# The second block's first modulation product, with 32 stationary columns in four partition groups for 64 in two

## What is computed

```python
def second_block(x, c, ada_w, ada_b, ...):
    cond = jax.nn.silu(c)                                  # 1 x 1024
    for layer in range(2):
        mod = (jnp.dot(cond, ada_w[layer]) + ada_b[layer])[:, None, :]   # 1024 x 6144
        sh1, sc1, g1, sh2, sc2, g2 = jnp.split(mod, 6, axis=-1)
        u = x * (1.0 + sc1) + sh1
        mix = _mixer(u, ...)
        x = _layernorm(ALPHA * x + (1.0 + g1) * mix, ...)
        u = x * (1.0 + sc2) + sh2
        ff = dense or mixture of experts, by layer
        x = _layernorm(ALPHA * x + (1.0 + g2) * ff, ...)
```

## Time and profile before

| | us |
|---|---|
| median of 3 runs | 2465.17 |
| lowest, highest | 2464.88, 2468.07 |
| the profiled execution | 2463.09 |
| its span, first to last instruction | 2461.4 |

### The profile page before, as it was taken

One profiled execution on the slowest core, in us unless ns is written; L12 is line 12 of the kernel. 1 busy time (PEld: TensorE's weight loads), 2 busy tenths in 40 slices (PEclk: granted clock), 3 DMA queues, 4 the chain that ended last, 5 costly groups with the idle time before them and its releaser, 6 DMA issues.

```text
span 2461.4 us, 68582 instructions
## 1 busy us (share of the span) xinstructions
PE 2197.1 (89%) x31915; PEld 1811.6 (74%) x31915; DVE 694.4 (28%) x1496; ACT 141.7 (6%) x270; POOL 160.5 (7%) x196
## 2 busy tenths in 40 slices
PE   6699989999999979779997977898898989899895
PEld 2478687777767768447764844798898979798895
DVE  7765242222222231343324224201011010101013
ACT  1101010000000000100000010000000000000000
POOL 8970000000000000000000000000000000000000
PEclk8899969999999969789998987899999999899998
DMA  9953569999999983237656322498988989898881
GB/s 345 301 180 120 189 208 353 394 395 394 394 395 394 394 297 128 95 133 257 247 205 222 120 103 81 160 335 308 336 301 301 327 305 343 299 347 302 313 313 67
DMA packets 304875, 658.36 MB, mean 267 GB/s; under 512 B 19844, under 2 KB 40852, under 8 KB 304660
## 3 DMA queue, kind: packets, MB, share of 16 engines
q1 hardware_dynamic: 295072, 646.99, 71.9%
q0 software_dynamic: 1456, 5.24, 0.7%
q10 hardware_dynamic: 8132, 2.72, 0.5%
HBM read 653.88 MB, written 1.05 MB: 266 GB/s over the span
## 4 chain that ended last, share of the span: by engine, by line
PE 78%; DMA 8%; DVE 6%; issue 5%; SPq 1%; ACT 1%; DVEq 0%; ACTq 0%
PE ps L1432 77%; DMA ring<-in_w_down_dram 8%; DVE arena L771 2%; PE ps L1440 2%; SPq L320 1%; DMA x<-in_x_dram 0%; DVE stat L870 0%; ACT hT L543 0%; DVE arena L1315 0%; ACTq L494 0%; DVE x L848 0%; DVE x L879 0%; DVE x L850 0%; DVEq L771 0%; DVE arena L1365 0%
## 5 line engine op out<-in xcount | busy, mean ns | idle before, releaser
L1432 PE MATMUL ps<-arena,ring 128*64 128x96 f32 (+2 forms) x25216 | 1010.5, 242 | 73.9 <-issue 70.4
L1432 PEld LDWEIGHTS ps<-arena,ring 128*64 128x64 f32 (+1 forms) x25216 | 991.1, 140 | 101.0 <-issue 95.3
L1432 PE MATMUL ps<-hT,ring 128*128 128x256 f32 x1616 | 353.5, 382 | 19.6 <-ACT hT L543 19.6
L1432 PEld LDWEIGHTS ps<-hT,ring 128*128 128x128 f32 x1616 | 308.6, 191 | 61.9 <-DVE stat L813 17.9
L1432 PE MATMUL ps<-ring,arena 128*64 128x512 f32 (+1 forms) x880 | 285.0, 616 | 17.4 <-DMA ring<-in_w_down_dram 14.9
L1432 PE MATMUL ps<-arena 128*128 128x128 f32 (+7 forms) x1296 | 242.2, 359 | 26.9 <-DVE arena L1143 11.4
L1168 DVE TENSOR_TENSOR arena<-arena,ps 128x384 f32<-128x384 f32 (+1 forms) x80 | 38.5, 481 | 741.3 <-PE ps L1432 741.3
L1432 PEld LDWEIGHTS ps<-ring,arena 128*64 128x64 f32 (+1 forms) x880 | 109.1, 164 | 175.2 <-issue 171.4
L1432 PEld LDWEIGHTS ps<-arena 128*128 128x128 f32 (+4 forms) x1296 | 166.7, 202 | 81.5 <-issue 50.4
L596 ACT ACTIVATE arena<-ps 128x384 f32<-128x384 f32 (+1 forms) x80 | 34.5, 432 | 1289.6 <-PE ps L1432 1289.6
L459 POOL TENSOR_SCALAR arena<-arena,starts,relD 128x256 f32<-128x256 f32 x64 | 92.1, 1446 | 9.2 <-DVE arena L737 5.9
(11 more groups left out here) (300 smaller groups left out, 892.0 us busy)
## 6 DMA issues: line engine op xcount, KB each, us to landing
ring<-in_moe_w_gate_dram SPq DMA_DIRECT2D x40, 2048.0 KB, 9.5
ring<-in_moe_w_up_dram SPq DMA_DIRECT2D x40, 2048.0 KB, 9.6
ring<-in_moe_w_down_dram SPq DMA_DIRECT2D x40, 2048.0 KB, 9.4
ring<-in_w_gate_dram SPq DMA_DIRECT2D x32, 2048.0 KB, 19.8
ring<-in_w_up_dram SPq DMA_DIRECT2D x32, 2048.0 KB, 19.7
ring<-in_w_down_dram SPq DMA_DIRECT2D x32, 2048.0 KB, 19.0
ring<-in_w_in_dram SPq DMA_DIRECT2D x18, 2048.0 KB, 10.5
ring<-in_w_ada_dram SPq DMA_DIRECT2D x12, 2048.0 KB, 20.4
```

The costliest lines, as they stand in the source:

```text
L1432: ins = pe.matmul(*args, **kw)
```

## The change

`ada_chunks` cuts each block of 128 features into four quarters of 32 columns, which go to partitions 0, 32, 64 and 96 of the same column of the same bank, where it cut it into two halves of 64. A chunk then has 128 matmuls in place of 64, or 256 recorded pairs in place of 128. Loops, slots, banks, semaphores, loads and what DVE reads stay as they are.

```diff
+QUARTER = 32
...
                     for f in range(4):
                         for k in range(KD):
-                            for c in range(2):
-                                at = f * P + c * HALF
-                                last = mm(ps[c * HALF:(c + 1) * HALF, bank, f:f + 1],
-                                          slot(s, KD, CH)[:, k, at:at + HALF], csT[:, 1, k:k + 1],
+                            for c in range(4):
+                                at = f * P + c * QUARTER
+                                last = mm(ps[c * QUARTER:(c + 1) * QUARTER, bank, f:f + 1],
+                                          slot(s, KD, CH)[:, k, at:at + QUARTER], csT[:, 1, k:k + 1],
                                           start=(k == 0), stop=(k == KD - 1))
```

## The result

| us | before | after |
|---|---|---|
| median (runs) | 2466.62 (4) | 2504.07 (4) |
| lowest, highest | 2464.88, 2474.83 | 2500.83, 2510.45 |
| profiled execution | 2463.09 | 2500.83 |
| its span | 2461.4 | 2499.1 |

A forecast was written before the change was run, and what follows sets the result against it. TensorE was taken to bound the kernel, with every chunk on the path. Pairs (+22.9 us) and code stalls (+19.3) made +42.2 on the profiled 2463.09, 2505.3; that run lying 2.1 below the median, 2507.4 was predicted, range 2484 to 2535.

The forecast's parts named there:

- A packet for 128 pairs: In all chunks, one instruction packet was to hold 128 pairs, so a chunk's code goes from one packet to two.
- the floor: In the chunks, issuing a weight load and a matmul was to take 29.9 ns a pair at either clock.
- the low bound: In the chunks, a pair's time goes with its columns: 15 ns at full clock, 26.7 at half, less if four loads overlap.
- rival 3: In the chunks, four loads overlap and code keeps ahead: 6.7 ns a pair at full clock, 13.3 at half; -31 us, 2434; 5%.
- The pairs' term: Over all twelve chunks, twice the pairs at 29.9 ns each were to add 22.9 us.
- The price of a stall: In chunks under weight loads, TensorE was to wait 1.9 us for each packet asked for; +19.3 us together.
- with the DMA mostly idle it costs nothing: In chunks without weight loads, such as chunk 2, fetching the added code was to bring no stall.
- If a chunk at half clock gets shorter: In chunks at 1.2 GHz, a shorter time was to show the forecast wrong in the main; about 9.5 us was expected under load.
- chunks at or under 3.8 us: In the changed profile, chunks this short were to be the sign of rival 3.
- 1 (code in time): In the chunks, code arrives in time and only the pairs count: +22.9 us, 2488; 15%.
- 2 (53.3 ns whatever the width): In chunks at half clock, a pair costs 53.3 ns at any width and nothing stalls: +81 us, 2546; 12%.
- 4: In the chunks, pairs go with their columns, two loads overlap, no stall: no difference, about 2466; 4%.

The follow-up runs named there:

- doubled halves: The kernel before with its halves of 64 columns, each sum made twice, so a chunk has 256 pairs; 2554.03 us.
- the best edit: Against the kernel before: condition column stationary, 128 weight columns moving, four partition groups, plus 110 small idle transposes ahead of the second expert loop; 2438.36 us, 0.9877.
- shifted: The kernel before with 18 extra small transposes (36 instructions) where TensorE waits, ahead of the second expert loop; 2480.9 us, 1.0056.
- the loop of two passes: The changed kernel with each chunk's quarters in a hardware loop run twice with the same results, one small matmul ahead and one behind; 2554.59 us.

## Why the prediction was right, and where it was wrong

- **The path.** Right: a chunk is on the path for all its length, nothing ahead absorbs the delay, behind chunk 12 next to nothing changes. +37.1 us at the transposes, +37.7 at the end of the span.
- **A packet for 128 pairs.** Right, to the packet: 12 more for 1536 more pairs. The Trainium skill, Runtime: NRT & Kernel Launch, Instruction fetch mechanics, gives blocks of 256 instructions fetched one after the other; this agrees (a packet for 128 recorded pairs of two instructions). Its "mostly hidden", which the prediction weighed, doesn't hold here: 63.7 us of stalls.
- **The price of a pair.** Wrong, and the step that failed is the floor: 29.9 ns for two forms was read as a floor on issuing. It was column time divided by the groups, and a rest of 2.4 to 4.7 ns at full clock that stays unexplained. Measured were 9.1 and 14.7 ns, below the low bound of 15 and 26.7 and near rival 3's 6.7 and 13.3. The pairs' term is -30.5 us for +22.9. The mechanism of rival 3 was true in this half. The prediction had read the half clock's 53.3 ns as column time; at full clock the same law gives 26.7, and the floor was built on the 3.2 ns that are missing, and on a second form that has 64 stationary columns as well.
- **The price of a stall.** Wrong in size by its use of the first: it took a packet's 5.7 us under load less 3.8 us of pairs. The distance was right (measured mostly 5.5 to 6.5 under load, up to 6.8), but the pairs fill 1.2 to 1.9 of it, so a stall is 4 to 5.4 us. And "with the DMA mostly idle it costs nothing" was wrong, as a packet then takes some 3.6 us, 1.5 to 2.5 of them idle. The row it was read from, the pairs of 29.8 ns from 363.06, could not show this: 128 of those last 3.8 us, just longer than the packet. Stalls come to 63.7 us together, for 19.3.
- **Why the sum held.** The terms are off by -53.4 and +44.4 us, and cancel to within 9. That is not luck alone: a cheaper pair only moves time from pairs to stalls, and the prediction had said so ("the packets then set the pace"; some 12 us less for a pair of 20 ns). It is luck in this: a later chunk was to take 5.7 us for a packet and 3.8 for pairs of 29.9 ns, and took 6.2 and 3.3 to 3.9, the second a packet as well. The wrong price of a pair came out near the time of a packet without load, which the prediction had not read anywhere. So chunks 9 to 12 came out at 38.1 for 38.2. Chunks 1 to 3, and 7 and 8, took 7.5 us less than forecast: in 1 and 3 the first 240 to 256 pairs had no gap in them, and 7 and 8 had a DMA share of 0.41. The lower clock behind the stalls adds about 3, within the 0 to 4 left for it.
- **The sign by which it would be wrong.** "If a chunk at half clock gets shorter" didn't occur. Yet "chunks at or under 3.8 us" for rival 3 couldn't show it, since the stalls hide it. The pair's time within a run of pairs was the sign to name.
- **The rivals.** 1 (code in time) falls with the gaps; 2 (53.3 ns whatever the width) with 14.7; 4 with both. 3 was right on the array and wrong on the code, and the forecast the other way round.

Still open: what makes a packet come at 3.6 and at 6 us (the DMA's own time or the queueing behind weights), the 6 us in the second expert loop with doubled halves, and the rest of a pair's time at full clock. A loop over the chunk's own blocks, so that its code stays at hand, was not tried as a version of its own.

## What to carry to other kernels

Of straight code made of very small matmuls count the packets: 128 pairs each, some 6 us under weight loads and some 3.6 without, and a stretch is the longer of its pairs and its packets, less the packets that are at hand when it starts (two here). To use the array's groups, give each instruction more to do (128 moving columns, four groups, a column of one as the stationary side) rather than cut the same work into more of them; here the granted clock stayed higher as well. And whoever adds or removes code ahead of a hot loop looks at how many instructions stand in its first packet before judging the edit: it was worth 10 to 13 us here, beside 29 us for the best edit.

## What the runs showed that was not expected

- Loads of the stationary side in four partition groups overlap nearly fourfold: 107 ns a pair of 64 columns in one group, 14.7 of 32 in four, at half clock. The Trainium skill, TensorEngine Tiling (Array Packing), Theoretical Speedup, gives up to 4x for a small side of at most 32. Per column it is 1.67 to 0.46 ns here, 3.6x, so the trace comes near it.
- At a DMA share of 0.02 packets of code still come only every 3.5 to 4.0 us, and under weight loads mostly every 5.5 to 6.5.
- A loop's place in its packets costs 2.3 to 2.4 us a pass in the mean of six, with the same instructions inside: 109.9 us before, 112.2 shifted.
- In the loop of two passes the second had no gap at all: code of two packets stays at hand. The first expert loop of the kernel before holds about five (5 packets come from 363 to 432 us) and asks for none from 432 to 872; the second, with 19 a pass, fetches them anew each time. How much stays lies between.
